# Hyena block of a two-block transformer: the matrices of both transforms loaded once, the inverse in two sets of four tiles, the second order begun among the turned tiles

## What is computed

```
u = dwconv_centred(x @ w_in, w_short)
v, g1, g2 = jnp.split(u, 3, axis=-1)
z = v
for o, gate in enumerate((g1, g2)):
    k_f = jnp.fft.rfft(two_sided_kernel(filt[:, o, 0], filt[:, o, 1]), n=n, axis=0)
    z_f = jnp.fft.rfft(z, n=n, axis=1)
    y = jnp.fft.irfft(z_f * k_f, n=n, axis=1)[:, :length]
    z = gate * (y + d_bias[o] * z)
return z @ w_o
```

## Time and profile before

| | us |
|---|---|
| median of three runs | 2246.6 |
| lowest and highest | 2245.58, 2247.1 |
| the profiled execution | 2249.11 |
| its span, first to last instruction | 2247.2 |
| matmul engine busy in the span | 2119.4 (94%) |
| DVE, POOL, ACT busy | 1322.2, 936.5, 837.6 |
| last matmul of the Hyena input GEMM starts | 1648.78 |
| DVE takes the first tile out of the inverse, order 0 and order 1 | 1695.03, 1764.03 |

### The profile page before, as it was taken

How to read it: one execution, slowest core, us unless ns; L and a number is a source line. 1 busy time by engine, 2 the same in 40 slices (tenths; PEclk the granted TensorE clock), 3 DMA queues, 4 the chain that set the end, 5 groups by cost and what they waited for, 6 DMA issues and landing times.

```text
span 2247.2 us, 23701 instructions
## 1 busy us (share of the span) xinstructions
PE 2119.4 (94%) x9729; PEld 1731.7 (77%) x9729; DVE 1322.2 (59%) x1665; ACT 837.6 (37%) x1209; POOL 936.5 (42%) x401
## 2 busy tenths in 40 slices
PE   8999989889999998999999999999988799999997
PEld 5677768767888887787877877878877687887786
DVE  7665871635234543465377776455677837777653
ACT  4623455552122224566243333333321324333322
POOL 4352135544444445112434444453676443444443
PEclk9998879989999998999999999989999989999998
DMA  6322112211222221111212223214231221232221
GB/s 208 137 87 75 38 38 79 90 56 67 103 94 94 94 94 54 41 49 56 76 57 94 96 94 110 94 57 178 94 141 52 98 76 59 99 104 95 95 94 38
DMA packets 34560, 194.05 MB, mean 86 GB/s; under 512 B 3903, under 2 KB 4495, under 8 KB 14932
## 3 DMA queue, kind: packets, MB, share of 16 engines
q1 hardware_dynamic: 34452, 192.54, 24.5%
HBM read 178.82 MB, written 13.64 MB: 86 GB/s over the span
## 4 chain that ended last, share of the span: by engine, by line
PE 61%; DVE 24%; ACT 9%; POOL 3%; issue 2%; DMA 0%; ACTq 0%; SPq 0%; DVEq 0%; POOLq 0%
PE ps L133 55%; DVE TMP L162 9%; DVE TMP L168 6%; PE ps L132 5%; ACT WH L149 4%; POOL X L156 1%; ACT TMP L150 1%; DVE TMP L156 1%; ACT PAD L149 1%; PE ps L141 1%; DVE ps L168 1%; DVE Y L156 1%; DVE X L156 1%; DVE VG L156 1%; DVE X L168 1%
## 5 line engine op out<-in xcount | busy, mean ns | idle before, releaser
L156 POOL TENSOR_TENSOR WL<-W,WH 128x2048 fp32r<-128x2048 f32 (+3 forms) x156 | 667.6, 4281 | 1012.9 <-ACT WH L149 1012.9
L133 PE MATMUL ps<-HH,WL 128*128 128x512 f32 (+1 forms) x1408 | 556.5, 395 | 29.9 <-DVE HL L168 8.1
L133 PE MATMUL ps<-HL,WH 128*128 128x512 f32 (+1 forms) x1408 | 546.0, 388 | 0.0
L133 PE MATMUL ps<-HH,WH 128*128 128x512 f32 (+1 forms) x1408 | 545.9, 388 | 0.0
L149 ACT ACTIVATE WH<-W 128x2048 fp32r<-128x2048 f32 (+2 forms) x150 | 278.5, 1857 | 321.3 <-PE ps L133 321.3
L133 PEld LDWEIGHTS ps<-HH,WL 128*128 128x128 f32 x1408 | 270.4, 192 | 101.5 <-issue 34.8
L133 PEld LDWEIGHTS ps<-HH,WH 128*128 128x128 f32 x1408 | 269.5, 191 | 53.9
L133 PEld LDWEIGHTS ps<-HL,WH 128*128 128x128 f32 x1408 | 270.3, 192 | 50.4 <-issue 0.2
L156 DVE TENSOR_TENSOR MRL<-MID,MRH 128x512 fp32r<-128x512 f32 x76 | 177.4, 2366 | 162.4 <-ACT MRH L149 162.4
L162 DVE TENSOR_SCALAR TMP<-PAD,PAR 128x512 f32<-128x512 f32 x88 | 208.9, 2374 | 76.3 <-ACT PAD L149 76.3
L133 PE MATMUL ps<-MRH,WL 128*128 128x512 f32 x608 | 238.4, 392 | 4.5 <-DVE TMP L168 2.2
(11 more groups left out here) (355 smaller groups left out, 3377.2 us busy)
## 6 DMA issues: line engine op xcount, KB each, us to landing
W<-in_up SPq DMA_DIRECT2D x44, 1024.0 KB, 4.8
W<-in_down SPq DMA_DIRECT2D x22, 1024.0 KB, 4.8
W<-in_w_up SPq DMA_DIRECT2D x16, 1024.0 KB, 4.8
W<-in_w_down SPq DMA_DIRECT2D x16, 1024.0 KB, 4.8
W<-in_hy_in SPq DMA_DIRECT2D x12, 1024.0 KB, 4.8
kd<-STG SPq DMA_DIRECT2D x36, 256.0 KB, 2.0
KB<-kd SPq DMA_DIRECT2D x8, 1024.0 KB, 5.0
W<-in_win_ag SPq DMA_DIRECT2D x4, 1024.0 KB, 4.8
```

What stands on the lines that cost most here:

```text
L133: return self.eng.matmul(out, lhs, rhs, start=start, stop=stop)
L156: return QUIET if self.eng is None else self.eng.tensor_tensor(out, a, b, op)
```

## The change

- `dft_z` and `dft_i` are loaded, split and kept once for both orders. The second pair of chunks is gone from `CHUNKS`, and ACT, POOL and SP have no work on them in order 1. `w_used` of both is said in order 1 only.
- Of `dft_i`, POOL still makes the first half of the low part ahead of the products; DVE makes the second half in four pieces of 256 columns (`inverse_low`) between its products and low parts, and the odd steps of the inverse wait for their piece (`di`).
- Groups (m, c) are taken in the order of `GROUPS`; the real and the imaginary group of a pair follow each other on the matmul engine. In order 1 the pairs are (0,0), (1,0), (0,1), (1,1), and then as before.
- The inverse opens four banks, runs steps 0 to 3 over tiles 0 to 3, opens four more, and runs them over tiles 4 to 7. The first two tiles then do steps 4 to 6 together, and finish first.
- Among the last three transposes of order 0, the first four forward groups of order 1 are computed, those of (0,0) and (1,0). DVE does the product group (0,0) ahead of the low parts of tiles 6 and 7. The turned tiles are built in `TMP[4]` and `TMP[5]`, outside the ring.
- The two scalar_tensor_tensor operations of a tile become one of 512 elements that reads the bank's 256 twice. The gate products of order 1 are DVE's for tiles 3 and 7 only, and POOL's for the other six.
- There are four buffers for the filter spectra; the third and fourth lie in `W32[0]` and `W32[1]`. In order 1 each part has its own. The first `hy_o` chunk is loaded when all parts of order 1 have been read, POOL makes its low part in pieces of 512 columns, and ACT copies it between the high parts 3 and 4.

```diff
+GROUPS = [[(m, c) for m in range(4) for c in range(2)],
+          [(0, 0), (1, 0), (0, 1), (1, 1), (2, 0), (2, 1), (3, 0), (3, 1)]]
...
-                pss = [open_bank("zi", o, m) for m in range(8)]
...
-                for k in range(4):
-                    for m in range(8):
+                for q in range(0, 8, 4):
+                    for m in range(q, q + 4):
+                        pss[m] = open_bank("zi", o, m)
+                    for k in range(4):
+                        for m in range(q, q + 4):
+                            ins = istep(m, k)
+                        if q:
+                            ins.then_inc(*up(acc, ("y_used", o, k)))
+                for k in range(4, 7):
+                    for m in range(2):
+                        istep(m, k)
+                for m in range(8):
+                    for k in range(7 if m < 2 else 4, 8):
                         ins = istep(m, k)
...
+                    if o == 0 and m >= 3:
+                        turn_z(1, m - 3)
                 if o == 0:
+                    turn_z(1, 5)
+                    to_spectrum(1, 0, 0, 0)
+                    to_spectrum(1, 0, 1, 0)
                     turn_z(1, 6)
+                    to_spectrum(1, 1, 0, 0)
                     turn_z(1, 7)
+                    to_spectrum(1, 1, 1, 0)
...
+            def inverse_low(k):
+
+                n = CH["dft_i"][0]
+                p = slice(1024 + 128 * (k - 1), 1280 + 128 * (k - 1))
+                dve.wait_ge(*at("w_high", n))
+                dve.low(WL[n % 2][:, p], W32[n % 2][:, p], WH[n % 2][:, p]).then_inc(
+                    *up(w_low2, ("di", k), *[("w_low2", n)] * (k == 7)))
+
             for o in range(2):
-                weights(CH["dft_i"][o])
...
+                for i, (m, c) in enumerate(GROUPS[o]):
+                    products(o, m, c)
+                    if o and i == 0:
+                        z_low(1, 6)
+                        z_low(1, 7)
+                    if i == 3:
                         y_low(o, 0)
-                for k in range(1, 8):
+                    if i == 5 and o == 0:
+                        inverse_low(1)
+                    if i == 6:
+                        y_low(o, 1)
+                for k in range(2, 8):
+                    if k % 2 and o == 0:
+                        inverse_low(k)
                     y_low(o, k)
...
-                    dve.stt(v1, v1, db, ps[:, 0:256], ALU.mult, ALU.add).then_inc(*out())
-                    dve.stt(v2, v2, db, ps[:, 0:256], ALU.mult, ALU.add).then_inc(*out())
+                    dve.stt(both, both, db, ps[:, 0:256].unsqueeze(1).broadcast_to([128, 2, 256]), ALU.mult,
+                            ALU.add).then_inc(*out())
...
+            sp.wait_ge(*at("kbu", 1, 0))
+            sp.wait_ge(*at("kbu", 1, 1))
             load("xl", X[:], XD)
-            weights(*range(CH["hy_o"][2], len(CHUNKS)))
+            for m in (2, 3):
+                sp.wait_ge(*at("kbu", 1, m))
+            weights(*range(CH["hy_o"][0], len(CHUNKS)))
```

More of the change, by code:

```diff
@@ L59 @@
 CHUNKS += [("hy_in", i, 2048) for i in range(12)]
-for _o in range(2):
-    CHUNKS += [("dft_z", 0, 2048), ("dft_i", 0, 2048)]
+CHUNKS += [("dft_z", 0, 2048), ("dft_i", 0, 2048)]
 CHUNKS += [("hy_o", i, 2048) for i in range(4)]
@@ L240, in temporaries @@
             for o in range(2):
[L241 to L245, removed]
-                    for m in range(8):
-                        ring.add("zt", 1, m)
+                for m, c in GROUPS[o]:
+                    for i in range(4):
+                        ring.add("q", o, m, c, i)
         for k in range(8):
@@ L270, in build @@
         kd_stored = [sem(f"kd_stored{i}") for i in range(16)]
-        kb_land = [sem("kb_land0"), sem("kb_land1")]
+        kb_land = [sem(f"kb_land{i}") for i in range(4)]
         kx_land = sem("kx_land")
@@ L413, in blk, with turning, rows @@
             return slice(128 * i, 128 * i + 128)
+        def turning(o, j):
+            return TMP[4 + j % 2] if o else tmp("zt", 0, j)
+        def rows(o, m):
+            return m if o else m % 2
         def half(c):
@@ L475, in chunk @@
                 pe.wait_ge(*at("w_low", n))
-                if n in SHARED:
+                if n in SHARED and n not in CH["dft_i"]:
                     pe.wait_ge(*at("w_low2", n))
@@ new lines, in products @@
+            def products(o, m, c):
+                kb = KB[rows(o, m)]
+                kr, ki = kb[:, half(c)], kb[:, 1024 + 512 * c:1536 + 512 * c]
+                kr2 = kr if m else KX[o][:, half(c)]
+                pr, pi = bank("zf", o, m, 0, c), bank("zf", o, m, 1, c)
+                q = [tmp("q", o, m, c, i)[:] for i in range(4)]
+                dve.wait_ge(*at("kb", o, m))
+                dve.wait_ge(*at("zf", o, m, 0, c))
+                vacant("q", o, m, c, 0)
+                dve.tt(q[0], pr[:], kr, ALU.mult).then_inc(*out())
+                dve.wait_ge(*at("zf", o, m, 1, c))
+                vacant("q", o, m, c, 1)
+                dve.tt(q[1], pi[:], ki, ALU.mult).then_inc(*out(("yr", o, m, c)))
+                vacant("q", o, m, c, 2)
+                dve.tt(q[2], pr[:], ki, ALU.mult).then_inc(*out(("free", "zf", o, m, 0, c)))
+                vacant("q", o, m, c, 3)
+                if m == 0:
+                    dve.wait_ge(*at("kx", o))
+                dve.tt(q[3], pi[:], kr2, ALU.mult).then_inc(
+                    *out(("yi", o, m, c), ("free", "zf", o, m, 1, c), *[("kbu", o, m)] * c))
```

159 lines of the change are left out of this document (68 added, 91 removed).

## The result

The changed kernel takes 2236.6 us (median of four, 2233.09 to 2237.43) against 2246.85 of the kernel before beside it (2245.58 to 2248.12): 0.9953, 95% between 0.9938 and 0.9967. A second set of seven runs, against twelve of before, gave 2237.94 and 0.9960 [0.9945, 0.9975]. So it gained 8.4 to 10.3 us where 14.5 were forecast: the time lies inside the range of 2226 to 2239, above the point of 2232.1.

What follows compares the result with a forecast made beforehand. The prediction took DVE and POOL to bound the stretch from 1652 to 1790.6 us. Its terms, 4.0 + 9.7 - 0.5 + 1.3 = 14.5, gave 2232.1 us on the median of 2246.6, range 2226 to 2239.

Steps and rivals of the forecast that it cites:

- First order, 4.0: Input ready to first tile out of order 0's inverse: 4.0 us earlier, between 2.5 and 5.
- Between the orders, 9.7: First tile out of order 0 to the second order's stream: 29.7 us becomes 20.0, gain 9.7, between 8 and 10.5.
- twelve forward matmuls at 0.43 instead of 0.22 cost 2.5, of which DVE feels 1.5. I take 20.0: Between the orders: allowance for a fall of the clock, on a stream start of 19.3 us after the first tile.
- So DVE has its first product group at 18.2: Between the orders: DVE starts the second order's first product group 18.2 us after the first tile, ending it at 20.8.
- Second order, -0.5: Second order, product stream to first tile: 39.3 us becomes 39.8, between a loss of 2.6 and a gain of 2.5.
- The four pieces cost between 0 and 4.1 here. I take 2: Second inverse: POOL's low part of the first output matrix, in four pieces beside four DVE low parts, costs 2 us.
- the walk's 36.8: Second order: step-by-step sum at full clock from stream start to first tile, 56.1 - 19.3 = 36.8 us.
- Second inverse to the first chunk, 1.3: Second inverse to first output chunk, 26.6 us before: gain 1.3, with 1.9 to -0.3 by meetings of gates and low parts.
- (a): Everything is covered: no clock fall in the inverse's thin parts, pieces fall between low parts; gain 19.9, 2226.7 us; chance 0.14.
- (c): The second order's early start brings its stream no earlier after the inverse; only 4.0 is left, 2242.6 us; chance 0.07.
- (d): Slower: thin work keeps the matmul engine at 1.2 GHz through both inverses; 2268 us; chance 0.05.
- (b): The lower ends of all four terms together: gain 7.6, 2239 us; chance 0.16.

Runs made afterwards that it cites:

- no early start: The changed kernel with order 1's forward groups behind all eight transposes, and tiles 6 and 7 lowered ahead of DVE's products: 2234.9 us (0.9949).
- two operations: The changed kernel with two scalar_tensor_tensor operations of 256 a tile again instead of one of 512: 2237.59 us (0.9954).
- pieces later: Filled gap, with POOL's pieces of the first output matrix held back until ACT has made high part 3 of order 1: 2232.69 us (0.9945).
- filled gap: The changed kernel with the output matrix loaded in order 0 and eight unread 512-column matmuls in the wait ahead of tile 5's transpose: 2230.83 us (0.9929).
- one set: The changed kernel with the inverse in one set of eight tiles again, all banks opened first: 2236.28 us (0.9956).
- two experiments: The changed kernel with POOL's four pieces writing 2 columns instead of 512: 2233.55 us (0.9944); or with the output matrix loaded in order 0: 2232.61 us (0.9937).
- two sets alone: The kernel before with the inverse in two sets of four and nothing else: 2253.29 us against 2245.6 (1.0041).

## Why the prediction was right, and where it was short

- **What bounds it.** Right. The stretch follows DVE and POOL; the waits for banks and for turns are gone, and what lies behind just shifts (its length differs by 1.7).
- **First order, 4.0.** Right within its range, at 3.3. Taken back one at a time, the two sets cost 2.1 and the quarters' place 2.5; that is more than the 3.3 together, so they overlap. The term for a fall of the clock was needed: it fell in the thin part of the first inverse in every profile of a changed kernel. Where that fall lasted 3.4 us (no early start, two operations, pieces later) the first tile came at 42.0, and where it lasted 6.8 in a kernel with both at 42.4 to 42.6. The quarters were sized too small, at 0.35 each: they took 0.52 in the loop, 0.42 twice, and 1.49 beside POOL's additions:

```profile
1672.28 1.49 DVE L159 TENSOR_TENSOR WL<-W,WH 128x256 fp32r<-128x256 f32 x1
```

- **Between the orders, 9.7.** Too high: 7.4, below the lower end of 8. The step that was off first is "twelve forward matmuls at 0.43 instead of 0.22 cost 2.5, of which DVE feels 1.5. I take 20.0": the sum stood at 19.3, and 20.0 charges 0.7 of that 1.5. Measured is 22.3. The second is "So DVE has its first product group at 18.2". The clock cost 1.65, since filled gap and one set, both at 1.00 there, start the group at 23.4 and 23.5 instead of 25.1: that is 0.95 more than the 0.7 charged. The other 1.35 of the missing 2.3 is the walk itself, which at full clock gave 20.7 and not 19.3: even in filled gap DVE reached its first product at 19.0, not at 18.2, and the second group another 4.4 later, not 3.8, with waits of 0.25 and 0.40 that the sum had at nothing.
- **Second order, -0.5.** The mechanism was right, its size not: -2.4 and -3.1, just inside and beyond the lower end of -2.6. "The four pieces cost between 0 and 4.1 here. I take 2": they cost 2.8, by two experiments. That leaves 38.9 without them, 2.1 above the walk's 36.8, with no fall of the clock in either. (The walk's own sum has a slip: 45.7 + 1.4 + 5.8 is 52.9, not 53.1.) Low parts 2 and 3 took 3.55 instead of two of 1.23, and the one ahead of the last product group 1.72, together 1.6 more than the walk has; POOL's additions run beside them. That these 1.6 are on the chain is argued, not tested:

```profile
1733.36 3.55 DVE L159 TENSOR_TENSOR YL<-YF,YH 128x1024 fp32r<-128x1024 f32 x2
```

  "ACT's copy ... 1.3 late, mostly made up": made up in full where the pieces are gone, and passed on by a quarter of a microsecond between the two profiles where they are not.
- **Second inverse to the first chunk, 1.3.** Right: 1.0 and 1.35. With one more meeting, not two, but also a smaller gain from the single operation.
- **Rivals.** (a) fell with the clock and the pieces, (c) with the start at 22.3, (d) because the clock came back after 3.4 to 10.2 us in every profile. (b), the lower ends with a gain of 7.6, came nearer to the stretch's 8.6 and 9.55 than the forecast's 14.5: two unknown costs, the clock and the low parts beside POOL, came out near their dear ends together. That the time still lies in the range is the width of the range, not the sizes of its terms.
- **What is not shown.** No run puts back the removed loads alone. Taken back one at a time, the early start cost 1.8 to 2.8 in the end, the quarters' place 1.8 to 2.7, the single operation 0.3 to 1.3, the two sets and the split of the gates at most 1.0 each. How much of the 8.6 to 9.6 the loads are worth by themselves stays open.
- **What decides the clock.** Open. The same wait of 2.3 was followed by 0.50 in the changed kernel and by 1.00 in one set. No experiment here makes it fall or stay at will.

## What to carry to other kernels

Work on POOL that is moved should be moved to where DVE waits: the same four pieces cost 2.8 beside the low parts of the second inverse and nothing 5 us earlier. A reordering that removes a wait takes away the cover of whatever ran under it; two sets alone cost 6.8 here, and cost nothing with the loads gone. Where the matmul engine does thin work, charge the fall of the clock in full each time, and measure such a change over its own stretch, not over a kernel of 2.2 ms.

## What the runs showed of the hardware

DVE's subtraction of two SBUF tensors (1.23 for 1024 columns) and POOL's (1.25 to 1.4 for 512) slow each other almost to one after the other: 8.16 and 7.98 for four of each, begun 0.9 apart. The four low parts lost 3.2 by it. In the first order of the kernel before, POOL's low part in one piece of 5.59 took 4.1 from the low parts beside it (11.32, less three of 1.23 and, as in the changed kernel, 3.54 for a pair beside the additions). No run has one piece and four at the same place, so what the cutting itself does isn't shown.

With a wait of the matmul engine filled, the clock stayed at 1.00 there, and in both profiles with the fill it was at half in the second inverse, where that cost 1 us. In the changed kernel the clock fell behind waits of 1.99 and 2.31 with thin work around them; behind a wait of 2.32 at the same place it stayed at 1.00 in one set.
